# Down projection: the high parts of the weights by a converting DMA from POOL instead of ACT's copy

## What is computed

```python
def swiglu(h, w_gate, w_up, w_down):
    return (jax.nn.silu(h @ w_gate) * (h @ w_up)) @ w_down

        x = x + mix @ w_out[l]

        x = x + swiglu(rmsnorm(x, norm2_g[l]), w_gate[l], w_up[l], w_down[l])
    return rmsnorm(x, norm_f_g)
```

## Time and profile before

| | |
|---|---|
| Median of 3 runs | 798.29 us (797.98 to 798.69) |
| Profiled execution, its own time | 798.42 us |
| Its span, first to last instruction | 796.5 us |
| PE busy | 779.7 us (98%) |
| DVE busy | 372.3 us (47%) |
| ACT busy | 254.4 us (32%) |
| POOL busy | 24.4 us (3%) |
| Mean traffic | 95 GB/s |
| Mean granted clock of PE | 0.994 of full speed |

### The profile page before, as it was taken

The page is one execution under the profiler, slowest core; times in us unless marked ns, Lnnn a source line. Parts: engine busy times, 40 slices in busy tenths (PEclk is TensorE's granted clock), DMA queues, the critical chain, the costliest instruction groups (busy, mean ns, idle before and its releaser), DMA issues.

```text
span 796.5 us, 9542 instructions
## 1 busy us (share of the span) xinstructions
PE 779.7 (98%) x3851; PEld 640.6 (80%) x3851; DVE 372.3 (47%) x576; ACT 254.4 (32%) x421; POOL 24.4 (3%) x45
## 2 busy tenths in 40 slices
PE   6999999999899999999999999999999999999996
PEld 6988888788576788888889988888888888888885
DVE  4688434357777443342547434334443444223224
ACT  6444221244455332332333332332332233123111
POOL 4000000012100000000000000000000000000000
PEclk9999999999999999999999999999999999999999
DMA  8434333211111034332331332233332233332402
GB/s 227 122 103 136 129 106 105 62 46 53 54 54 39 16 106 159 106 105 106 109 103 54 107 98 69 98 106 106 105 107 89 74 103 107 115 96 66 146 0 107
DMA packets 61916, 75.64 MB, mean 95 GB/s; under 512 B 3680, under 2 KB 49840, under 8 KB 61872
## 3 DMA queue, kind: packets, MB, share of 16 engines
q1 hardware_dynamic: 61872, 75.02, 29.4%
HBM read 72.92 MB, written 2.10 MB: 94 GB/s over the span
## 4 chain that ended last, share of the span: by engine, by line
PE 93%; DVE 2%; issue 2%; ACT 1%; DMA 1%; POOL 1%; SPq 0%; POOLq 0%; DVEq 0%; ACTq 0%
PE bank L1148 29%; PE bank L1150 28%; PE bank L1149 28%; PE bank L1369 1%; PE bank L1337 1%; PE bank L1354 1%; DMA stage<-in_w_in 1%; PE bank L1298 1%; PE bank L1160 1%; PE bank L1311 1%; POOL head_rs L428 0%; PE bank L1344 0%; PE bank L1272 0%; PE bank L1291 0%; DVE hT_lo L710 0%
## 5 line engine op out<-in xcount | busy, mean ns | idle before, releaser
L1148 PE MATMUL bank<-hT_hi,w_hi 128*128 128x512 f32 (+1 forms) x680 | 261.4, 384 | 2.8 <-DVE hT_lo L710 2.4
L726 DVE TENSOR_TENSOR w_lo<-stage,w_hi 128x1024 fp32r<-128x1024 f32 x125 | 152.4, 1224 | 228.8 <-ACT w_hi L469 220.3
L1150 PE MATMUL bank<-hT_hi,w_lo 128*128 128x512 f32 (+1 forms) x680 | 257.1, 378 | 0.0
L1149 PE MATMUL bank<-hT_lo,w_hi 128*128 128x512 f32 (+1 forms) x680 | 257.0, 378 | 0.0
L469 ACT ACTIVATE w_hi<-stage 128x1024 fp32r<-128x1024 f32 x127 | 133.4, 1053 | 132.7 <-PE bank L1150 127.3
L1148 PEld LDWEIGHTS bank<-hT_hi,w_hi 128*128 128x128 f32 x680 | 128.8, 189 | 27.5 <-issue 3.0
L1150 PEld LDWEIGHTS bank<-hT_hi,w_lo 128*128 128x128 f32 x680 | 128.7, 189 | 23.9
L1149 PEld LDWEIGHTS bank<-hT_lo,w_hi 128*128 128x128 f32 x680 | 128.8, 189 | 21.8
L1148 PE MATMUL bank<-w_hi,aT_hi 128*128 128x512 f32 x176 | 68.5, 389 | 0.0
L1149 PE MATMUL bank<-w_lo,aT_hi 128*128 128x512 f32 x176 | 68.5, 389 | 0.0
L1150 PE MATMUL bank<-w_hi,aT_lo 128*128 128x512 f32 x176 | 68.5, 389 | 0.0
(11 more groups left out here) (175 smaller groups left out, 770.8 us busy)
## 6 DMA issues: line engine op xcount, KB each, us to landing
stage<-in_w_in SPq DMA_DIRECT2D x21, 1024.0 KB, 5.2
stage<-in_w_gate SPq DMA_DIRECT2D x11, 1024.0 KB, 5.4
stage<-in_w_up SPq DMA_DIRECT2D x11, 1024.0 KB, 5.3
stage<-in_w_down SPq DMA_DIRECT2D x22, 512.0 KB, 4.4
stage<-in_w_out SPq DMA_DIRECT2D x4, 1024.0 KB, 5.1
x_nat<-in_x SPq DMA_DIRECT2D x4, 512.0 KB, 5.4
stage<-in_w_br_mlstm SPq DMA_DIRECT2D x4, 512.0 KB, 3.5
stage<-in_w_br_fox SPq DMA_DIRECT2D x4, 512.0 KB, 4.5
```

Source lines behind the costliest of these rows:

```text
L726: dve.tensor_tensor(ring(w_lo, g), staged(g), ring(w_hi, g).bitcast(F32), ALU.subtract).then_inc(lo_split, 1)
L1148: pe.matmul(o, a_hi, b_hi, start=first, stop=False)
L1149: pe.matmul(o, a_hi, b_lo, start=False, stop=False)
L1150: return pe.matmul(o, a_lo, b_hi, start=False, stop=last)
```

## The change

For the 22 granules of the down projection ACT no longer copies. POOL queues a second transfer of the same 512 KB of w_down from HBM, straight into the `w_hi` buffer; since the target's type is F32R, the transfer converts. It waits for the same count of `used` as the copy did, and counts up a semaphore of its own per ring buffer, `hi_landed`. SP still loads the float32 values into `stage`. DVE, which used to wait for ACT's `hi_split`, now waits for the stage and for `hi_landed`. The 22 transfers stand in POOL's queue between the rstd of the second norm and that of the last.

```diff
+        hi_landed = [sem(f"hi_landed{i}") for i in range(RING)]
...
+        def down_block(g):
+
+            half, f = down[g - G_DOWN]
+            return w_d[f * P:(f + 2) * P, half * HALF:(half + 1) * HALF].rearrange("(k p) c -> p k c", p=P)
+
+        def ring_count(g):
+
+            return (g - G_DOWN) // RING + 1
...
             rows_rstd(1)
+            for g in range(G_DOWN, N_GRAN):
+                pool.wait_ge(used, g - RING + 1)
+                pool.dma_start(ring(w_hi, g), down_block(g)).then_inc(hi_landed[(g - G_DOWN) % RING], 16)
             rows_rstd(2)
...
             def split_hi(g):
-                if g >= N_GRAN:
+                if g >= G_DOWN:
                     return
                 wait_stage(act, g)
                 if g >= RING:
                     act.wait_ge(used, g - RING + 1)
...
             def split_lo(g):
                 if g >= N_GRAN:
                     return
-                dve.wait_ge(hi_split, g + 1)
+                if g < G_DOWN:
+                    dve.wait_ge(hi_split, g + 1)
+                else:
+                    wait_stage(dve, g)
+                    dve.wait_ge(hi_landed[(g - G_DOWN) % RING], 16 * ring_count(g))
```

## The result

| | before | after |
|---|---|---|
| Median | 798.27 us (797.63 to 798.78, 8 runs) | 800.09 us (798.38 to 800.96, 8 runs) |
| Profiled execution, its span | 798.42, 796.5 us | 800.32, 798.6 us |
| ACT busy | 254.4 us | 231.4 us |
| POOL busy | 24.4 us | 40.4 us |
| w_down's transfers to `stage`, to landing | 4.4 us | 5.8 us |

The ratio is 1.0023, with a 95% interval of 1.0013 to 1.0034: the change costs 1.8 us, between 1.0 and 2.7. The forecast was 4.8 us.

What follows compares the result with a forecast made beforehand. PE was taken to bound the kernel, exposed only at granule 21 in the tail. The terms 0 + 0 + 3.1 (stall) + 1.7 (clock) = 4.8 us gave 803.1 us; range 799.6 to 806.5.

Steps and rivals of the forecast that it cites:

- What bounds the kernel, and where it is exposed: PE is full in the down projection; only granule 21 at the tail has little cover, 1.50 us against 16.3 elsewhere.
- The cover of 1.50 us: At granule 21, row block 0: DVE's subtraction ends at 771.02, PE needs the granule at 772.52.
- 22 copies off ACT, worth 0: Down projection: about 23 us of ACT's time removed, worth 0 since PE doesn't wait for ACT there.
- Steady part, cost 0: Granules 0 to 19: DMA share rises from 0.30 to about 0.60, landing up to 15 us is hidden, cost 0.
- Rival D: DMA engines bound the stage if converting costs over 2.3 times a plain transfer; 820 us at three times; chance 0.05.
- The landing time: Granule 21's transfer at the tail: taken as 5.5 us, giving a PE stall of 3.1 us, bounds 1.0 and 5.1.
- L: Landing time of granule 21's converting transfer at the tail, taken as 5.5 us; the stall is L - 2.4 us.
- The clock: Behind the tail's stall: PE's granted clock falls just as PE resumes, costing 1.7 us more.
- The formula 770.1 + L: Time at which PE can start granule 21 at the tail: 768.70 + L + 1.4, instead of 772.52.
- rival B: At the tail, stall of 1.5 to 2.5 us without the clock's fall: 799.8 to 800.8 us; chance 0.26.

Runs made afterwards that it cites:

- the plain transfer by POOL: Changed kernel, but POOL's 22 transfers go unconverted to float32 scratch buffers and ACT copies from there: 810.6 us (one run).
- the queue comparison: Unconverted transfers into scratch buffers, then ACT's copy, issued by POOL in one kernel, by ACT in the other: last transfer 4.34 and 3.79 us, totals 810.6 and 816.6.
- the kernels with two additions: Changed kernel plus two additions on dead data on DVE before granule 21's subtraction, measured twice: 802.72 us (1 run), 802.75 us (4 runs).
- the one with 2.12 us of idling: Changed kernel, but ACT issues the transfers, unconverted into scratch buffers, and copies from there: 816.6 us (one run).

## Why the prediction was wrong, point by point

- **What bounds the kernel, and where it is exposed: right.** The cover of 1.50 us at granule 21 is the one place that matters. The kernel with granule 21 alone changed and the one with it alone left out show this from both sides. One reading was too generous and harmless: three full granules, 16.3 us, lie between release and use only up to granule 18. Granule 19 is freed 5.44 us before 20, at about 757.8, and is needed at 769.80, 12.0 us later. The landing time of 4.8 us is far below that too.
- **22 copies off ACT, worth 0: right.** 21 transfers cost and gain nothing (0.9998).
- **Steady part, cost 0: right.** The DMA share is 0.66 against the 0.60 estimated for equal cost, because converting takes 1.2 times the engines' time, and SP's own loads of w_down land after 5.8 us in place of 4.4. Both have cover. Rival D needed more than 2.3 times.
- **The landing time: the step that failed.** L was taken as 5.5 us, the middle of 4.0 and 5.1 plus 1 for POOL. It is 4.35, and the stall 2.0 us in place of 3.1. The middle allowed 0.55 us for converting, where the plain transfer by POOL shows 0.0; the 1 us for POOL is 0.55 by the queue comparison, and the base from ACT's queue 3.79 instead of 4.0. That is 0.55 + 0.45 + 0.2 = 1.2 us too much, which is the whole difference. The rest of the chain held: 0.14 us that POOL starts later than ACT did (768.84 for 768.70) and 1.28 from DVE's start to PE's, 1.42 where 1.4 was taken. The formula 770.1 + L gives 774.45 with the L measured; PE went on at 774.47.
- **The clock: the second step that failed, a term added to the stall.** The forecast has 1.7 us for a fall behind the stall, and nothing of it was paid in the trace of the changed kernel, where the clock stayed at 1.00. The size was about right where it does fall (1.6 us at the end of the span), and the kernels with two additions, with a stall of the forecast's size and a fall, take 4.8 and 5.2 us more than the kernel before beside them, where 4.8 was forecast. But the forecast took it that the clock falls behind such a stall, and a stall of that length doesn't settle it: of two stalls of 3.1 us, one had the fall and one had not. Nor is it settled that it stays behind 2.0 us: it held in both traces that show such a stall and fell in the one with 2.12 us of idling.
- **What came of it.** The outcome was rival B, 799.8 to 800.8, to which I gave 0.26 against 0.44. The 1.15 us too much in L and the 1.7 us of the clock are 2.85 of the 3.0 us by which 4.8 is more than the measured 1.8; the rest is within the interval. That 800.09 lies inside the stated range of 799.6 to 806.5 says little, since the range holds the cases with and without the fall.
- **What the page that was cited gives.** The Trainium skill, DMA: Bandwidth & Descriptors (Anatomy of one DMA), gives 2.0 us plus bytes over 436 GB/s, an estimate of 3.2 us for this transfer. The trace does not agree: from POOL's issue to its user it took 4.35. The first-byte latencies on that page of the Trainium skill (Specifications), 1 us for the software path against 0.6, make 0.4 of difference by the queue; the traces show 0.55 for the last and 0.8 for the median. Converting adds none on landing in the runs, by the rows above.
- **The spread.** The changed kernel's eight runs reach from 798.38 to 800.96 us, 2.6 wide. That is no sign of a clock that falls at the tail in some of them: 24 runs of the kernel before, which has no stall there, reach from 797.0 to 799.88. The four runs with two additions reach from 801.09 to 804.69; only one of them has a trace, so how many of them had the fall isn't known.

## What to carry to other kernels

Moving work off an engine that nothing waits for gains nothing, and moving it to a DMA exchanges a short delay (here 1.05 us) for a long one. Look for the one granule whose buffer is freed latest relative to its use, often the last of a stage with another loop order, and compare the landing time (here 4.35 us) with what the old step took plus its cover (1.05 + 1.50 us) before all else. If that granule gets a buffer that is already dead, the transfer costs nothing that could be measured here. And where a second term, such as the clock, may or may not come on top of a stall, give the case without it its own weight: it moves the sum by the whole term (1.7 of 4.8 us here), and the stall's length alone doesn't tell.

## What was not expected of the hardware

- A converting transfer of 512 KB lands as soon as a plain one from the same queue (4.35 and 4.34 us for the last, 4.8 and 4.7 in the median), though it takes 1.2 times the DMA engines' time and nearly twice the packets (5984 and 3168).
- The landing time of the last transfer by POOL is steady: between 4.24 and 4.54 us in the seven traces where PE waits for it, and POOL is busy 0.72 us for each, 0.92 for the first.
- The clock's fall behind a pause of PE is not a function of the pause's length alone: held at 2.94 us, fallen at 2.12 and 2.95, and mixed, six fallen to five held, at the same 1.97 us of the same place in the program.
- What a fall of the clock costs in the end differs by place: 1.6 us of the span at the tail, and 0.6 to 0.7 us at 209 us.
